# Window attention of the later layers regrouped into pairs of chunks with alternating row halves

## The reference

```python
WINDOW = 128        # SEQ = 512, ATTN_HEADS = 8, ATTN_KV_HEADS = 2, head dim 64
def sliding_window_attention(q, k, v, sinks):
    ...
    kk = jnp.concatenate([jnp.concatenate([jnp.zeros_like(kb[:, :1]), kb[:, :-1]], axis=1), kb], axis=2)
    ...
    s = jnp.einsum('bnqkgd,bnskd->bnkgqs', qb, kk) * (D ** -0.5)
    ...
    mx = jnp.maximum(jnp.max(s, axis=-1, keepdims=True), sink)
    p = jnp.exp(s - mx)
    denom = jnp.sum(p, axis=-1, keepdims=True) + jnp.exp(sink - mx)
    o = jnp.einsum('bnkgqs,bnskd->bnqkgd', p / denom, vv)

def token_mixer(h, ...):
    z = h @ w_in        # parts: mq, mk, mv, mo, gates, aq, ak, av
    qk = silu(causal_dwconv(concat(mq, mk)) + b)       # four taps
    ...                                                # mLSTM, then concat and w_out
```

## Time and profile before

| what | value |
|---|---|
| time, median of 3 runs | 3371.57 us (3367.11 to 3378.58) |
| the profiled execution's own time | 3373.94 us |
| its span, first to last instruction | 3372.1 us |
| mean granted TensorE clock | 0.870 |
| PE busy | 2781.9 us (82%) |
| DVE busy | 1150.6 us (34%) |
| ACT busy | 877.5 us (26%) |
| POOL busy | 889.8 us (26%) |
| chain that ended last, share of the span | PE 62%, DMA 21%, DVE 7%, ACT 3%, POOL 3% |

### The profile page before, as it was taken

The page is one execution under the profiler, slowest core; times in us unless marked ns, Lnnn a source line. Parts: engine busy times, 40 slices in busy tenths (PEclk is TensorE's granted clock), DMA queues, the critical chain, the costliest instruction groups (busy, mean ns, idle before and its releaser), DMA issues.

```text
span 3372.1 us, 34593 instructions
## 1 busy us (share of the span) xinstructions
PE 2781.9 (82%) x13172; PEld 1933.9 (57%) x13172; DVE 1150.6 (34%) x1930; ACT 877.5 (26%) x1567; POOL 889.8 (26%) x562
## 2 busy tenths in 40 slices
PE   7898897999847777777767739998999789989998
PEld 5687875777722222222222217766887667668876
DVE  4332234622131211211111245454443355444433
ACT  2223222332201111111111122343333323433323
POOL 3122223534111111111111122213444322234433
PEclk9686878999868878887888869989999889889999
DMA  4011221022449999999999952102322221122221
GB/s 161 31 50 38 75 84 60 26 100 87 180 181 416 411 407 412 414 405 408 405 407 404 406 202 69 68 33 75 100 100 75 83 73 51 51 75 83 92 100 63
DMA packets 133322, 586.87 MB, mean 174 GB/s; under 512 B 15136, under 2 KB 62544, under 8 KB 106960
## 3 DMA queue, kind: packets, MB, share of 16 engines
q1 hardware_dynamic: 116864, 553.64, 42.1%
q10 hardware_dynamic: 9808, 23.15, 1.9%
q0 software_dynamic: 6528, 8.44, 0.7%
HBM read 579.06 MB, written 14.78 MB: 176 GB/s over the span
## 4 chain that ended last, share of the span: by engine, by line
PE 62%; DMA 21%; DVE 7%; ACT 3%; POOL 3%; issue 2%; ACTq 1%; SPq 1%; POOLq 1%; DVEq 0%; PEldq 0%
PE ps L323 36%; DMA wide<-in_moe_w 19%; PE ps L915 6%; PE ps L1344 4%; PE ps L1328 3%; PE ps L586 2%; POOL ring_r L301 2%; PE ps L614 2%; PE ps L600 1%; DVE xn L357 1%; PE ps L1320 1%; PE ps L839 1%; DMA arena<-normed_rows,arena 1%; PE ps L2007 1%; SPq L1275 1%
## 5 line engine op out<-in xcount | busy, mean ns | idle before, releaser
L301 POOL TENSOR_TENSOR ring_r<-ring,ring_r 128x1024 fp32r<-128x1024 f32 (+2 forms) x288 | 694.5, 2444 | 1424.9 <-ACT ring_r L295 1246.3
L1328 PE MATMUL ps<-wide,arena 128*32 128x512 f32 x2048 | 346.9, 811 | 255.9 <-DMA wide<-in_moe_w 253.1
L323 PE MATMUL ps<-ring_r,xnT_r 128*128 128x512 f32 (+2 forms) x1552 | 496.4, 401 | 37.4 <-POOLq L255 24.6
L323 PE MATMUL ps<-xnT_r,ring_r 128*128 128x512 f32 x1536 | 496.2, 398 | 13.7 <-POOLq L255 7.4
L323 PEld LDWEIGHTS ps<-ring_r,xnT_r 128*128 128x128 f32 (+1 forms) x1552 | 327.4, 222 | 92.0 <-issue 35.1
L323 PEld LDWEIGHTS ps<-xnT_r,ring_r 128*128 128x128 f32 x1536 | 291.9, 190 | 86.9 <-issue 15.5
L1328 PEld LDWEIGHTS ps<-wide,arena 128*32 128x32 f32 x2048 | 67.0, 130 | 459.2 <-DMA wide<-in_moe_w 266.3
L323 PE MATMUL ps<-ring_r,arena_r 128*128 128x512 f32 x1248 | 302.3, 401 | 16.0 <-DVE arena_r L2319 10.5
L295 ACT ACTIVATE ring_r<-ring 128x1024 fp32r<-128x1024 f32 (+2 forms) x288 | 273.6, 1024 | 121.2 <-DMA ring<-in_w_down 60.3
L323 PE MATMUL ps<-xn_r,ring_r 128*128 128x512 f32 x768 | 301.9, 393 | 0.0
L323 PEld LDWEIGHTS ps<-ring_r,arena_r 128*128 128x128 f32 x1248 | 238.1, 193 | 74.9 <-issue 25.0
(11 more groups left out here) (301 smaller groups left out, 3515.8 us busy)
## 6 DMA issues: line engine op xcount, KB each, us to landing
wide<-in_moe_w SPq DMA_DIRECT2D x192, 2048.0 KB, 13.1
ring<-in_w_in SPq DMA_DIRECT2D x27, 2048.0 KB, 7.9
ring<-in_w_up SPq DMA_DIRECT2D x22, 2048.0 KB, 8.4
ring<-in_w_down SPq DMA_DIRECT2D x10, 2048.0 KB, 7.8
ring<-in_w_out SPq DMA_DIRECT2D x6, 2048.0 KB, 8.4
ring<-in_w_ret_branch SPq DMA_DIRECT2D x2, 2048.0 KB, 9.5
arena<-expert_rows ACTq DMA_DIRECT2D x4, 1024.0 KB, 9.2
attn_spill<-arena ACTq DMA_DIRECT2D x2, 1056.0 KB, 4.0
```

Of the source, the lines that this page charges most:

```text
L301: nc.gpsimd.tensor_tensor(ring_r[:, q % 2, cols], ring[:, q % 2, cols], ring_r[:, 2 + q % 2, cols].bitcast(F32), ALU.subtract).then_inc(ha ...
L323: ins = nc.tensor.matmul(bank, left, right, start=(start and k == 0), stop=(stop and k == 2))
L1328: res.append(nc.tensor.matmul(ps[g * CAP:(g + 1) * CAP, bank, :], xT[:, c, :], w[:, c, :], start=(c < 4), stop=(c >= KC - 4), tile_positio ...
```

## The change

`attend_pair_scores_pe` issues the scores of two neighbouring attention chunks, 2p and 2p+1, with the heads of the two row halves in turn. `project_steps` no longer spreads 48 steps. After every eighth product chunk, the first time after chunk 5, there is one group: values of pair p-2, turn of pair p-1, scores of pair p, for p from 0 to 9, so after chunks 5, 13, 21, ... 77. DVE and ACT handle both attention chunks of a pair at each step. ACT's work of the last values step (tile copy, Silu, Sigmoid) goes with the group after chunk 77.

```diff
--- before.py
+++ after.py
@@ -586,6 +586,22 @@
                 ins = nc.tensor.matmul(ps[:, A.bank0 + n % 2, j * (k1 - k0):(j + 1) * (k1 - k0)], A.q(hh)[:, i * P:(i + 1) * P],
                                        A.k(hh)[:, k0:k1], start=True, stop=True)
             ins.then_inc(Z.scores_ready, 1)
+
+        def attend_pair_scores_pe(pe, A, p):
+
+
+            pair = (2 * p, 2 * p + 1)
+            if p:
+                pe.wait_ge(Z.scores_taken, 2 * p)
+            for j in range(len(range(*A.chunks[2 * p][1].indices(HEADS)))):
+                for n in pair:
+                    i, heads, keys, _ = A.chunks[n]
+                    hh = range(*heads.indices(HEADS))
+                    k0, k1 = keys[0][0].start, keys[-1][0].stop
+                    ins = nc.tensor.matmul(ps[:, A.bank0 + n % 2, j * (k1 - k0):(j + 1) * (k1 - k0)], A.q(hh[j])[:, i * P:(i + 1) * P],
+                                           A.k(hh[j])[:, k0:k1], start=True, stop=True)
+                    if j + 1 == len(hh):
+                        ins.then_inc(Z.scores_ready, 1)
 
         def attend_turn_pe(pe, A, n):
             i, heads, keys, _ = A.chunks[n]
@@ -1714,16 +1730,8 @@
         def project_steps():
 
 
-            W = len(window.chunks)
-            beside = [("scores", 0)]
-            for n in range(W):
-                if n + 1 < W:
-                    beside.append(("scores", n + 1))
-                beside.append(("turn", n))
-                if n:
-                    beside.append(("values", n - 1))
-            beside.append(("values", W - 1))
-            first, spread = 5, 76
+            W = len(window.chunks) // 2
+            first, apart = 5, 8
             chunk = 0
             for n in range(J.mv.stop):
                 if job_unit(n) is None:
@@ -1734,12 +1742,18 @@
                     if n >= J.qk.start:
                         if chunk == 2:
                             yield "rot", 2 * NT - 1
-                        while beside and chunk >= first + (3 * W - len(beside)) * spread // (3 * W):
-                            yield beside.pop(0)
+                        p, off = divmod(chunk - first, apart)
+                        if off == 0 and 0 <= p <= W + 1:
+                            if p >= 2:
+                                yield "values", p - 2
+                            if 1 <= p <= W:
+                                yield "turn", p - 1
+                            if p < W:
+                                yield "scores", p
                         chunk += 1
                 if 1 <= n <= 2 * NT - 1:
                     yield "rot", n - 1
-            assert not beside
+            assert first + apart * (W + 1) < chunk
 
         def rot_pe(pe, m):
             pe.wait_ge(Z.roped, m + 1)
@@ -1801,11 +1815,13 @@
                 elif what == "rot":
                     rot_pe(pe, k)
                 elif what == "scores":
-                    attend_scores_pe(pe, window, k)
+                    attend_pair_scores_pe(pe, window, k)
                 elif what == "turn":
-                    attend_turn_pe(pe, window, k)
+                    for n in (2 * k, 2 * k + 1):
+                        attend_turn_pe(pe, window, n)
                 elif what == "values":
-                    attend_values_pe(pe, window, k)
+                    for n in (2 * k, 2 * k + 1):
+                        attend_values_pe(pe, window, n)
 
         def rope_tile_dve(v, n):
             cos = table("cos_nat").rearrange("p (i d) -> p i d", i=NT)
@@ -1874,11 +1890,13 @@
                 elif what == "gate":
                     gate_rows_dve(v, link, k)
                 elif what == "scores":
-                    attend_mask_dve(v, link, window, k)
-                    if k == len(window.chunks) - 1:
+                    for n in (2 * k, 2 * k + 1):
+                        attend_mask_dve(v, link, window, n)
+                    if n == len(window.chunks) - 1:
                         window_sinks_dve(v)
                 elif what == "turn":
-                    attend_keep_dve(v, window, k)
+                    for n in (2 * k, 2 * k + 1):
+                        attend_keep_dve(v, window, n)
             window_end_dve(v, link)
 
         def project_act(a):
@@ -1910,12 +1928,13 @@
                     if i == 1 and q + 1 >= 2:
                         high_act(a, q + 1)
                 elif what == "scores":
-                    attend_exp_act(a, window, k)
-                    if k == len(window.chunks) - 1:
+                    for n in (2 * k, 2 * k + 1):
+                        attend_exp_act(a, window, n)
+                    if n == len(window.chunks) - 1:
                         window_end_act(a)
-                elif what == "values" and k % window.per_tile == window.per_tile - 1:
-                    attend_mixed_act(a, window, k // window.per_tile)
-                    if k == len(window.chunks) - 1:
+                elif what == "values" and (2 * k + 2) % window.per_tile == 0:
+                    attend_mixed_act(a, window, 2 * k // window.per_tile)
+                    if 2 * k + 2 == len(window.chunks):
                         nc.scalar.activation(Y.qk, Y.qk, ACT.Silu)
                         nc.scalar.activation(Y.mo, Y.mo, ACT.Sigmoid)
```

## The result

The changed kernel took 3380.65 us (median of 18 runs, 3376.31 to 3385.01), the kernel before 3371.54 (18 runs beside it). The ratio is 1.0026, interval [1.0018, 1.0033]. Forecast was 3380.7. Two more measurements of the same kernel, each beside the kernel before, gave 1.0011 [1.0000, 1.0023] and 1.0023 [1.0012, 1.0033]: 9.1, 3.0 and 7.7 us in the three, so the change costs some 3 to 9 us. The total came out as forecast, but in part by luck: the stages took less than forecast and what follows them more, and the two errors largely cancelled.

A forecast was written before the change was run, and what follows sets the result against it. PE was taken to bound the stage's middle, DVE and ACT nearly its first third, with PE, ACT and POOL tied at the end. 2.3 + 3.9 + 1.7 + 1.2 = 9.1 us on 3371.57 gave 3380.7; range 3367 to 3391.

The forecast's parts named there:

- What pairing saves on PE: Attention scores on PE: two opposite row halves run at once, saving 1.23 us a pair, 9.0 us per layer.
- saved edges: Scores steps on PE: even if nothing overlapped, a pair saves one set of edges, 0.42 us.
- Beside the qk jobs: First third of the stage: DVE and ACT bound it, PE idles 8.2 us, gain lost; first layer 0.7 us later.
- both chunks: Pair 2 on DVE: small operations of both chunks take 1.75 or 2.31 us while POOL works, instead of about 0.17.
- Beside mo and mv: Later jobs of the stage: PE saves 5.3 us, new waits and edges take most back, in all -1.4 us.
- about 1.8: Before job 19: PE's wait in the kernel before, taken to grow to 3.4 us, adding 1.5.
- The wait of 1.2 for the turn of pair 6: Beside mo and mv: PE waits for maxima delayed by POOL's conversion of unit 4, adding 1.2 us.
- The tail: Stage end: Silu and Sigmoid ahead of unit 5's high half delay POOL and the barrier; stages 2.3 and 3.9 us longer.
- +2.3 of the second layer: Stage end, second layer: POOL ends at 2872.9 instead of the stage's end at 2870.6, so 2.3 us later.
- The clock in the mo jobs: After PE's 8.2 us idle, second layer: clock at 1.2 GHz for about 3.5 us, costing 1.7 us.
- The clock in the mLSTM: Start of the mLSTM: a longer idle PE before it makes the first matmuls slow, 0.6 us per layer.

The follow-up runs named there:

- e3: Changed kernel with chunks reordered so both chunks of a pair have heads of the same row half; 3385.73 us, ratio 1.0043.
- e1: Changed kernel with Silu and Sigmoid moved behind the high half of unit 5 on ACT; 3367.53 us, ratio 0.9988.
- e2: Kernel before, no pairs, its attention spread cut from 76 to 74 chunks, so the last values step comes earlier; 3382.29 us, ratio 1.0030.
- The filler: Changed kernel plus 18 unused product matmuls on PE at the end of the projection stage; measured twice, 3379.18 and 3381.80 us.
- e11: Second measurement of the changed kernel plus 18 unused product matmuls at the projection stage's end; 3381.80 us, ratio 1.0023.
- e5: First measurement of the changed kernel plus 18 unused product matmuls at the projection stage's end; 3379.18 us, ratio 1.0012.
- e10: Changed kernel with Silu and Sigmoid late, ACT's jobs before exps of groups after a sixth or seventh chunk, and groups placed by hand; 3336.66 us, ratio 0.9891.
- e9: Kernel before, single chunks, ACT taking the ending job before a step that stands after its sixth or seventh chunk; 3364.32 us, ratio 0.9971.
- e6: e1 with ACT taking the ending job before a group's exps, PE and DVE order kept; 3347.65 us, ratio 0.9910.

## Why the prediction was right, and where it was not

- **What pairing saves on PE.** Right, a little low: 10.1 us per layer in the windows against 9.0. A pair takes 1.14 us, as "about 1.2" said. e3 shows that the overlap is the reason for some 7 of the 10; the other 3 are the saved edges, which the prediction priced at 0.42 a pair.
- **Beside the qk jobs.** The chain on DVE and ACT came out as counted: from the first mask (2767.15) to the first mo product (2802.44) 35.3 us, forecast 35.35. The idle PE before it was 6.1, not 8.2, since PE itself arrived later: turns waited 0.66 and 1.85 for exps, and the group at 2790.56 ran slower (1.58 for a pair, mean clock 0.68). Lines 659 and 660 were slow for the first chunk of pair 2 (1.43 and 2.32) but less so for the second (0.96 and 0.17), since POOL was done at 2788.57: "both chunks" was half right. In the first layer the mo jobs start 0.65 later than before, forecast 0.7.
- **Beside mo and mv.** The gain was priced too low. Forecast -1.4, and the 1.7 of the clock on top. From the first mo product to PE's last it was 74.15 and is 71.80: -2.35, with some 1.2 of low clock in it, so -3.5 without. In the first layer it was 75.75 and is 72.03, -3.7. The waits before job 19 (2.9, forecast 3.4) and job 22 (0.7, forecast 0.9) are there, the first against the 1.22 of the earlier trace rows and not "about 1.8". The wait of 1.2 for the turn of pair 6 did not come; the other 0.9 of the second layer is not accounted for.
- **The tail.** The mechanism was right: e1 takes it away and e2 makes it without pairs. Its size on the stage was not. Counted from the first mask of the second layer, PE ended 1.2 earlier than forecast, POOL followed after 4.58 instead of 5.0, and the mLSTM began 0.2 after POOL, where it used to begin 0.8 after ACT (0.6 less); I had not counted that last step. These 2.2 us turn the +2.3 of the second layer into +0.1.
- **The clock in the mo jobs.** It fell after the stop, as forecast: the window from 2802.40 to 2805.90 stands at 0.66, where before it was 1.00. At 2 x 3.5 x 0.34 = 2.4 us of low clock that costs 1.2, forecast 1.7.
- **The clock in the mLSTM.** The term that failed: "A longer idle PE before the mLSTM makes its first matmuls slow: 0.6 per layer". The rests are 3.0 and 3.4 longer, and with them not the first matmuls alone but the whole pattern of low clock over the next 150 us changed (37 / 41 to 49 / 48 us). I priced the few matmuls at the edge and not the stretch behind them. The 3.0 and 3.4 rest on one profile of the kernel before.

So the stages were over-priced by 7.8 us (7.9 forecast, 0.1 found) and what follows them under-priced by 5.3 (1.2 forecast, 6.5 found). That their sum met the measured time was luck: with the stages alone put right the forecast would have been 1.3 us slower instead of 9.1, with what follows them alone put right 14.4. The 6.6 found in the profiles is also 2.5 short of the 9.1 between the medians, and the repeats gave 3.0 and 7.7. The Trainium skill's rule that an idle gap puts the clock back to half (TensorE: Matmul & The Clock Gate, HAM oscillation) agrees with the first matmul: 2.04 after 4.79 idle, 1.09 after 1.77 or 0.75 idle. It does not account for the low clock further on. The filler shows that closing the gap does not keep the clock up through the mLSTM.

What stays open is why the low clock in the mLSTM takes one of several patterns. Over the table, the rest of the second layer goes with the low time (486.8 at 27 us, 487.0 to 490.4 at 34, 494.6 at 48), but e11 and e5 are one kernel with two patterns. No run here controlled it, so that the low clock makes the rest longer, and that the change makes the clock low, is argued and not shown.

The expected gain went into PE's idle time at three places: ACT's exps of a group ahead of the end of a job, with DVE's taps behind them (6.1 and 2.9 us), the two functions ahead of unit 5's conversion (4.6), and the slower mLSTM after that. e10 shrinks the stop of 6.1 to two of 4.3 together and takes the 2.9 and the 4.6 away. It is 27.7 us below e9's single chunks on the same chip (3364.32 to 3336.66), the placing of its groups included. What pairs alone are worth, once ACT takes jobs first and the functions come late, is read from e6 and e9: 0.9910 against 0.9971, some 20 us, though from two sets of runs.

## What to carry to other kernels

When a gain is made on one engine, look in the other engines' streams for what stands ahead of the work that returns a buffer: grouping steps puts two or four operations there where one stood. Take the job that frees the busy engine's bank first and the work with slack second; here that order was worth 10 us without the change (e9) and some 26 with it (e1 to e6, 0.9988 to 0.9910). Operations that belong to the next stage, such as an activation with its table load, go behind what another engine needs for this stage's barrier: worth 13 us here (e1).

## What the runs showed of the hardware

- Score matmuls of 64 rows in opposite row halves ran at the same time: eight in 1.14 us, eight of one half in 1.99.
- Operations on 2 columns took DVE 1.43, 2.32 and 0.96 us while POOL subtracted in fp32, and 0.17 without. The Trainium skill (SBUF — State Buffer, two separate sides) calls the port pair that the two engines share an exclusive lock held for a whole instruction. The longest, 2.32, is about one POOL operation of 9.40 / 4 = 2.35, and all three end within 0.1 us of where, by an even division of its four, a POOL operation ends, which agrees.
- With PE busy for 48.56 of 50 us, the granted clock still averaged 0.75 to 0.83 at the start of the mLSTM. Low time over 150 us lay between 27 and 49 us across these kernels, and one and the same program had 34 and 44.
- The kernel before had medians of 3371.5, 3372.2, 3377.8 and 3373.9 us in the four sets of runs, 0.2% apart, so a change of that size is read only against runs of the same set.
